# Second block: half the in-projection and all gate products dealt out by k steps between small products, the mask as contraction rows, the gate bias added by VectorE

## The chip, the cores and the metric

The kernel runs on one core of a Trainium2 chip, all in float32. Its time is the device time of the whole program in microseconds. Engines are TensorE (PE; PEld is its weight load), VectorE (DVE), ScalarE (ACT), GpSimd (POOL) and SyncE (SP).

## The reference

Two transformer blocks of depth 2 run one after the other on 256 tokens of width 1024. The first (adaptive norms, attention, a mixture of 32 experts) is untouched. Cut to what matters, a layer of the second is

```
h = rmsnorm(x, norm_g)
u_a, v_a, z_a, c_q, c_kv, k_r, z_b, q_c, k_c, v_c, g_c, z_c, gate_logits = split(h @ w_in)
y_a = gelu(u_a) * (mask(w_s) @ layernorm(gelu(v_a)) + b_s) * silu(z_a)
y_b = chunk_causal_attention(q(c_q), k(c_kv, k_r), v(c_kv)) * silu(z_b)      # 8 heads of 96
y_c = rmsnorm(gla(q_c, k_c, v_c, g_c)) * silu(z_c)                            # 4 heads, chunks of 64
gates = sigmoid(gate_logits + b_gate)                                         # 3 x 1024
x = x + (sum_n gates[n] * (y_n @ w_branch[n])) @ w_out
```

In y_b a query sees a key if the key's chunk of 64 is not later than its own.

## The kernel before

The 256 rows are two tiles of 128 (`LAT` = 2). A **unit** is one PSUM bank that TensorE fills and another engine takes: units A (`BANK_A`, three banks) are taken by ScalarE, units D (`BANK_D`, three) by VectorE, each ring in order. w_in and the other wide weights stream through a ring in SBUF: `stream` (L355 to L395) is the order, each item is 2 MB (a **chunk**: 1024 x 512, k-major in 8 slices), SyncE loads an item as soon as the last use of the item before it in its slot is done, and the second block uses `SLOTS2` = 4 of the six slots. The other two hold the opened gates `GS` and, on two partitions, the bias `BG`. Chunks 0, 1 and 2 of the eight in-projection chunks (`IN_CHUNKS`, the last 432 wide) give u_a, v_a and z_a, chunk 3 c_q, c_kv, k_r and the start of z_b.

TensorE's program of a layer (from L899) is written out by hand and sets the order of everything:

- in-projection (L906): 8 chunks x 2 tiles, a unit of 8 matmuls each (L912). A float32 matmul appears in the trace as two passes, so a unit is 16 rows of PE.
- rows: the spatial weight turned (L921), then gate units (L893, and L895 for the bias) and the spatial product (L928); for each tile the normalised latents are turned (L936, L937) and multiplied (L941, L942, L945), two gate units follow, and the heads' rows are turned (L951).
- heads: for each tile 8 heads in a pipeline of ten rounds: score (L961) with the chunk mask added by a product of the identity and a constant (L962), the probabilities' transposition (L969) one round later and the product with V (L979) two rounds later.
- GLA for each tile: L987 to L1036, with two of the gate units between.
- branches: one or two gate units, then for each branch the rows turned (L1048) and multiplied by w_branch (L1057); then the out-projection (L497, L1073).

In all 12 gate units of `gates` (L882):

```python
for k in range(KD):
    nc.tensor.matmul(u[:, :], HT2[:, k, tile * P:(tile + 1) * P], w[:, k, :], start=(k == 0), stop=False)
q, b0 = 32 * (c // BRANCHES), c % BRANCHES * 512
nc.tensor.matmul(u[:, :], C("ones")[q:q + 1, :].to_broadcast([1, P]), BG[q:q + 1, b0:b0 + 512], start=False,
                 stop=True).then_inc(s_unitA, 1)
```

ScalarE (from L1266) copies in-projection units, does Gelu, Silu, the square roots (L1109), the heads' exponentials (L1297) and opens each gate unit with a Sigmoid (L1264). VectorE (from L1935) normalises (L1956 to L2028), takes the maxima of the scores (L2041, L2043), copies what was turned (L2033, L2046) and adds up the branches (L2137 to L2142). POOL issues the layer's vector loads (L2300 to L2315).

## Time and profile before

| | |
|---|---|
| median of 3 runs | 2511.5 us (2511.03 to 2512.53) |
| profiled execution | 2511.9 us, span 2510.0 us |
| PE busy | 2068.1 us (82%) |
| DVE, ACT busy | 602.1 us (24%), 394.4 us (16%) |
| second block, layer 0 (first in-projection product to last branch product) | 1701.67 to 2065.42 |
| second block, layer 1 | 2107.48 to 2472.40 |

PE busy counts pipelined matmuls, with modelled ends: durations of neighbours overlap, so the pitch of a sequence is the difference of two starts. A bracket in a timeline row is the time in which the engine stood idle before that row, and who released it. PEclk is the TensorE clock that was granted, 1.00 for 2.4 GHz.

### The profile page before, as it was taken

The numbers are of one execution on the slowest core, as the hardware profiler recorded it, in microseconds if no ns is written. First come the engines' busy times: TensorE is split into PE (matmuls) and PEld (weight loads), VectorE is DVE, ScalarE is ACT, GpSimd is POOL, SyncE is SP. The second block draws the span as 40 slices with busy tenths as digits, with TensorE's granted clock in tenths as the row PEclk, the third lists the DMA queues.
The fourth block names the chain that finished last, engine by engine and source line by source line (L and its number), as shares of the span: only waits on it lengthen the run. The fifth ranks groups of instructions, "written<-read, shape, count | busy, mean of one in ns | idle before, by whom it ended". The sixth has DMA issues, their size and how long they took to land.

```text
span 2510.0 us, 20024 instructions
## 1 busy us (share of the span) xinstructions
PE 2068.1 (82%) x8105; PEld 958.4 (38%) x8105; DVE 602.1 (24%) x1340; ACT 394.4 (16%) x815; POOL 100.0 (4%) x148
## 2 busy tenths in 40 slices
PE   5999987778777776896877777759988899998898
PEld 1444434333332233553333333214435444444543
DVE  1234425200000004744000000020055231035322
ACT  1122410100000002331000000011222211031310
POOL 1001000100000001001000000001000001000000
PEclk8999998899999988997999998989988899998789
DMA  9257552799999997205999999966411134431020
GB/s 351 99 188 264 190 199 109 294 428 428 427 428 427 428 425 283 101 26 200 425 428 428 427 429 427 428 277 237 162 67 42 67 123 151 143 120 67 34 95 23
DMA packets 119727, 620.90 MB, mean 247 GB/s; under 512 B 8016, under 2 KB 10336, under 8 KB 95056
## 3 DMA queue, kind: packets, MB, share of 16 engines
q1 hardware_dynamic: 101664, 561.04, 55.6%
q0 software_dynamic: 12208, 37.54, 4.3%
q10 hardware_dynamic: 5760, 20.97, 2.2%
q8 instruction: 69, 1.13, 0.2%
q14 instruction: 26, 0.21, 0.0%
HBM read 594.30 MB, written 25.23 MB: 247 GB/s over the span
## 4 chain that ended last, share of the span: by engine, by line
PE 57%; DMA 31%; DVE 7%; ACT 2%; issue 2%; SPq 1%; ACTq 0%; POOL 0%; DVEq 0%; POOLq 0%
DMA ring<-in_w_up 28%; PE bank L680 11%; PE bank L912 9%; PE bank L893 7%; PE bank L760 5%; PE bank L1057 3%; PE bank L550 3%; PE bank L1073 2%; PE bank L814 2%; PE bank L634 2%; PE bank L610 1%; PE bank L497 1%; PE bank L895 1%; DMA ring<-in_w_ada 1%; DMA big<-mod_d 1%
## 5 line engine op out<-in xcount | busy, mean ns | idle before, releaser
L680 PE MATMUL bank<-ring,big 128*64 128x512 f32 x3072 | 743.8, 640 | 207.2 <-DMA ring<-in_w_gate 95.8
L680 PEld LDWEIGHTS bank<-ring,big 128*64 128x64 f32 x3072 | 261.0, 147 | 665.3 <-issue 630.0
L912 PE MATMUL bank<-ring,big 128*128 128x512 f32 (+1 forms) x512 | 220.1, 593 | 1.7 <-issue 1.7
L893 PE MATMUL bank<-ring,big 128*128 128x512 f32 x384 | 185.2, 639 | 0.0
L1885 DVE TENSOR_TENSOR big<-big,bank 128x512 f32<-128x512 f32 x32 | 22.0, 688 | 660.9 <-PE bank L680 660.9
L912 PEld LDWEIGHTS bank<-ring,big 128*128 128x128 f32 x512 | 98.7, 193 | 122.4 <-issue 122.4
L760 PE MATMUL bank<-ring,big 128*128 128x512 f32 x320 | 140.7, 599 | 0.0
L1091 ACT ACTIVATE big<-bank 128x512 f32<-128x512 f32 (+3 forms) x102 | 57.5, 576 | 461.1 <-PE bank L912 204.4
L893 PEld LDWEIGHTS bank<-ring,big 128*128 128x128 f32 x384 | 77.1, 206 | 99.7 <-issue 99.4
L497 PE MATMUL bank<-cst,big 128*128 128x128 f32 x176 | 31.5, 349 | 77.1 <-DVE big L1940 30.9
L1057 PE MATMUL bank<-ring,big 128*128 128x512 f32 x192 | 85.7, 605 | 4.4 <-ACT big L1091 4.4
L760 PEld LDWEIGHTS bank<-ring,big 128*128 128x128 f32 x320 | 61.0, 193 | 74.2 <-issue 74.2
L814 PE MATMUL bank<-ring,big 128*128 128x512 f32 x192 | 85.8, 602 | 0.0
L1890 DVE COPY big<-bank 128x512 f32<-128x512 f32 x32 | 22.1, 692 | 259.6 <-PE bank L680 259.6
L550 PE MATMUL bank<-ring,small 128*2 128x512 f32 x160 | 73.9, 593 | 8.1 <-DVE big L1392 7.8
L1213 ACT ACTIVATE big<-bank 128x512 f32<-128x512 f32 x32 | 19.1, 597 | 355.9 <-PE bank L672 355.9
L1218 ACT ACTIVATE big<-bank 128x512 f32<-128x512 f32 x32 | 19.1, 597 | 351.9 <-PE bank L680 351.9
L551 PE MATMUL bank<-ring,small 128*2 128x512 f32 x160 | 74.0, 593 | 0.0
L2243 POOL DMA_INDIRECT big<-h_d,slot_tok x32 | 30.8, 962 | 811.9 <-PE bank L672 772.0
L497 PEld LDWEIGHTS bank<-cst,big 128*128 128x128 f32 x176 | 27.5, 183 | 85.7 <-issue 51.9
L1177 ACT ACTIVATE big<-bank,small 128x512 f32<-128x512 f32 (+1 forms) x96 | 57.8, 612 | 6.2 <-DVE small L1538 6.2
L1226 ACT ACTIVATE big<-bank 128x512 f32<-128x512 f32 x32 | 19.1, 597 | 244.3 <-PE bank L680 244.3
(382 smaller groups left out, 1940.7 us busy)
## 6 DMA issues: line engine op xcount, KB each, us to landing
ring<-in_w_gate SPq DMA_DIRECT2D x64, 2048.0 KB, 18.4
ring<-in_w_up SPq DMA_DIRECT2D x64, 2048.0 KB, 19.9
ring<-in_w_down SPq DMA_DIRECT2D x64, 2048.0 KB, 19.6
ring<-in_w_in SPq DMA_DIRECT2D x26, 2048.0 KB, 7.8
ring<-in_w_ada SPq DMA_DIRECT2D x24, 2048.0 KB, 13.7
y_d<-big ACTq DMA_DIRECT2D x32, 512.0 KB, 10.3
ring<-in_w_qkv SPq DMA_DIRECT2D x6, 2048.0 KB, 19.9
ring<-in_w_branch SPq DMA_DIRECT2D x6, 2048.0 KB, 7.6
```

Source lines behind the costliest of these rows:

```text
L497: ins = nc.tensor.transpose(u[:, k * P:(k + 1) * P], rows[:, c:c + P], ident)
L550: nc.tensor.matmul(bank[0:2, :], cT[:, i, :], w0[:, i * 512:(i + 1) * 512], start=(i == 0), stop=(i == KD - 1))
L551: ins = nc.tensor.matmul(bank[64:66, :], cT[:, i, :], w1[:, i * 512:(i + 1) * 512], start=(i == 0), stop=(i == KD - 1))
L634: ins = nc.tensor.matmul(banks[6][64 * r:64 * r + 64, 0:256], ROWS[:, kt, v0:v0 + HD], PT(n)[:, i // 2, i % 2, 256 * r:256 * r + 256], sta ...
L680: ins = nc.tensor.matmul(bank[half * CAP:(half + 1) * CAP, :], lhs[:, k, half * CAP:(half + 1) * CAP], w[:, k * step + c0:k * step + c0 + ...
L760: ins = nc.tensor.matmul(u[:, :], hT(tile, k), w[:, k, :], start=(k == 0), stop=(k == KD - 1))
L814: ins = nc.tensor.matmul(u[:, :], hT(tile, k), wo[c][:, k, :], start=(k == 0), stop=(k == KD - 1))
L893: nc.tensor.matmul(u[:, :], HT2[:, k, tile * P:(tile + 1) * P], w[:, k, :], start=(k == 0), stop=False)
L912: ins = nc.tensor.matmul(u[:, 0:n], HT2[:, k, tile * P:(tile + 1) * P], w[:, k, :], start=(k == 0), stop=(k == KD - 1))
L1057: ins = nc.tensor.matmul(u[:, :], YT[:, k, tile * P:(tile + 1) * P], w[:, k, c * 512:(c + 1) * 512], start=(k == 0), stop=(k == 3))
L1091: nc.scalar.activation(dst, src, ACT.Copy, scale=scale).then_inc(s_outA, 1)
L1177: ins = nc.scalar.activation(pr[:, i * n:(i + 1) * n], sc[r][:, i * n:(i + 1) * n], ACT.Exp, bias=nm[:, h:h + 1], accum_out=rs[:, h:h + 1])
```

## The change

Of the in-projection, chunks 0, 1, 3 and 2 (in this order) stay whole units; the later four and all 12 gate units become **beside units**: a list `BESIDE` of 20 units, 160 steps of one k slice (one matmul, two passes). `beside(layer, n)` issues the next n steps wherever it is called, and the table `POINTS` says how many: 18 and 20 ahead of the turned heads, 4 (tile 0) or 3 (tile 1) a head, 4 to 10 at five places of GLA in either tile. Beside units have two banks of their own (`BANK_F`: the third of A, and one that only the first block used); units A of the second block go down to two banks. ScalarE copies the in-projection's beside units, VectorE adds the bias (now a broadcast of 128 x 3072 in SBUF) to the gates' ones, and ScalarE opens them later in place, 1024 wide. The bias products are gone.

The chunk mask becomes two more contraction rows of scores: `KMT` and `QMT` grow from 96 to 98 partitions, filled by three small DMAs on POOL's queue, and the mask product is gone. The latents of both tiles are normalised ahead of the spatial product, the gating of the spatial rows moves into tile 0's latents, Silu is done in three places, the branches' rows are turned earlier into two buffers, and the weight ring has three slots, since `BG` needs the room.

```diff
-SLOTS2 = 4
+SLOTS2 = 3
...
-        KMT = xc[0:MQK, :, :]...
+        MQX = MQK + LAT
+        KMT = xc[0:MQX, :, :]...
...
+        BG = spare[:, LAT * BRANCHES * D:(LAT + 1) * BRANCHES * D]
+        BANK_F = (banks[2], banks[7])
...
+        IN_ORDER = (0, 1, 3, 2, 4, 5, 6, 7)
+        BESIDE = [("in", *IN_CHUNKS[i], tile) for i in IN_ORDER[4:] for tile in range(LAT)]
+        BESIDE += [("gate", c, 512, tile) for c in range(2 * BRANCHES) for tile in range(LAT)]
...
+        POINTS = {"rows": (18, 20), "heads": (4, 3), "decay": (4, 6), "logs": (9, 10), "exps": (9, 9),
+                  "turned": (4, 4), "states": (6, 5)}
+        def bank_a(n):
+            return BANK_A[n % 3] if n < marks["second"] else BANK_A[(n - marks["second"]) % 2]
...
+            def beside(layer, steps):
+                for _ in range(steps):
+                    m, k = made[0] // KD % len(BESIDE), made[0] % KD
+                    n = made[0] // KD
+                    made[0] += 1
+                    kind, c, cols, tile = BESIDE[m]
+                    w, at_ = weights((kind, layer, c))
+                    u = BANK_F[n % 2]
+                    if k == 0 and n >= 2:
+                        pe.wait_ge(*beside_taken(n - 2))
+                    ins = nc.tensor.matmul(u[:, 0:cols], HT2[:, k, tile * P:(tile + 1) * P], ...
+                                           start=(k == 0), stop=(k == KD - 1))
...
-                    gates(layer, 2 - tile)
...
+                for i in (0, 1):
                     for tile in range(LAT):
+                        in_unit(layer, i, tile)
...
+                for tile in range(LAT):
+                    in_unit(layer, 3, tile)
+                spatial(0)
+                in_unit(layer, 2, 0)
+                spatial(1)
+                turned_at = latents_turn(0)
+                in_unit(layer, 2, 1)
+                pe.wait_ge(s_outA, turned_at)
+                latents_out()
+                turned_at = latents_turn(1)
+                beside(layer, POINTS["rows"][0])
+                heads_turn()
+                pe.wait_ge(s_outA, turned_at)
+                latents_out()
+                beside(layer, POINTS["rows"][1])
+                heads_turn()
                 taken("D")
+                pe.wait_ge(s_mask, 48 * (layer + 1))
...
-                            nc.tensor.matmul(u[:, n - P:n], ident, C("chunk"), start=False, stop=True,
-                                                  skip_group_check=True).then_inc(s_unitA, 1)
...
+                        if s < MH:
+                            beside(layer, POINTS["heads"][tile])
...
+                branches_at.append(branch_turn(1))
+                branch(layer, 0, branches_at[0])
+                branch(layer, 1, branches_at[1])
+                pe.wait_ge(s_dp, due(s_dp))
+                branches_at.append(branch_turn(2))
+                branch(layer, 2, branches_at[2])
...
+                    if kind == "in":
+                        act.wait_ge(s_fin, i + 1)
+                        nc.scalar.activation(PROJ[:, tile, c:c + cols], BANK_F[i % 2][:, 0:cols], ACT.Copy).then_inc(s_finA, 1)
...
+            def open_gates(layer, n):
+                act.wait_ge(s_finD, BESIDE_GATES * layer + 2 * LAT * (n + 1))
+                for tile in range(LAT):
+                    v = GS[tile][:, n * D:(n + 1) * D]
+                    nc.scalar.activation(v, v, ACT.Sigmoid).then_inc(s_sig, 1)
...
+                    if kind == "gate":
+                        dve.wait_ge(s_fin, i + 1)
+                        V.tensor_tensor(GS[tile][:, c * 512:(c + 1) * 512], BANK_F[i % 2], BG[:, c * 512:(c + 1) * 512],
+                                        ALU.add).then_inc(s_finD, 1)
...
-                dve.wait_ge(s_silus, due(s_silus, 3 * LAT))
...
+                    if tile == 0:
+                        dve.wait_ge(s_silus, due(s_silus, LAT))
+                        for i in range(LAT):
+                            uu = PROJ[:, i, C_U:C_U + BW]
+                            V.tensor_tensor(uu, uu, PROJ[:, i, C_ZA:C_ZA + BW], ALU.mult).then_inc(s_sgd, one(s_sgd))
...
+                load_vector(BG, t["b_gate_2"][layer], s_bg)
+                mask = t["consts"][:, CONST:CONST + MASK]
+                pool.wait_ge(s_h, marks["rows", layer])
+                pool.dma_start(KMT[MQK:MQX, :, :].rearrange("p h n -> p (h n)"), mask[0:LAT, :]).then_inc(s_mask, 16)
+                pool.wait_ge(s_sgd, LAT * (layer + 1))
+                for i in range(LAT):
+                    pool.dma_start(QMT[i][MQK:MQX, :, :].rearrange("p h n -> p (h n)"),
+                                   mask[LAT * (i + 1):LAT * (i + 2), 0:MH * P]).then_inc(s_mask, 16)
```

**TensorE, heads of tile 0.** L961 and L1044 are the scores, L962 the mask, L969 and L1050 the transposition, L979 and L1060 the product with V, L919 a beside step. Before:

```order
L961 MATMUL bank<-xc,big 128x128 [waits unit_taken_by_scalar]
L962 MATMUL bank<-cst 128x128
L969 MATMUL bank<-cst,big 128x128 [waits unit_taken_by_vector,unit_taken_by_scalar]
L979 MATMUL bank<-big 128x64 [waits o_unit_taken,unit_taken_by_vector]
L961 MATMUL bank<-xc,big 128x128 [waits unit_taken_by_scalar]
```

and now:

```order
L1044 MATMUL bank<-xc,big 128x128 [waits unit_taken_by_scalar]
L1050 MATMUL bank<-cst,big 128x128 [waits unit_taken_by_vector,unit_taken_by_scalar]
L1060 MATMUL bank<-big 128x64 [waits o_unit_taken,unit_taken_by_vector]
L919 MATMUL bank<-ring,big 128x512 [waits weights_slot0] x2
L919 MATMUL bank<-ring,big 128x432 [waits beside_unit_taken_by_scalar,weights_slot1]
L919 MATMUL bank<-ring,big 128x432 [waits weights_slot1]
L1044 MATMUL bank<-xc,big 128x128 [waits unit_taken_by_scalar]
```

A head is followed by four steps; the mask product is gone; a beside unit can begin in the middle of them, and there TensorE waits for ScalarE's copy of the unit two before.

**TensorE, tile 0 from the latents to the turned heads.** L936 to L945 and L953 to L965 are the latents, L893, L895 a gate unit, L951 and L973 the turned heads. Before, behind the latents' products:

```order
L893 MATMUL bank<-ring,big 128x512 [waits unit_taken_by_scalar,weights_slot1]
L893 MATMUL bank<-ring,big 128x512 x7
L895 MATMUL bank<-ring,cst 128x512
L893 MATMUL bank<-ring,big 128x512 [waits unit_taken_by_scalar,weights_slot2]
L893 MATMUL bank<-ring,big 128x512 x7
L895 MATMUL bank<-ring,cst 128x512
L951 MATMUL bank<-cst,big 96x128 [waits unit_taken_by_vector,vector_result_for_tensor]
L951 MATMUL bank<-cst,big 96x128 x3
L951 MATMUL bank<-cst,big 96x128 [waits unit_taken_by_vector]
```

and now, with the next tile's latents turned first:

```order
L953 MATMUL bank<-cst,big 128x128 [waits unit_taken_by_scalar,vector_result_for_tensor]
L953 MATMUL bank<-cst,big 128x128
L954 MATMUL bank<-cst,big 128x128
L919 MATMUL bank<-ring,big 128x512 [waits weights_slot1] x16
L919 MATMUL bank<-ring,big 128x512 [waits beside_unit_taken_by_scalar,weights_slot2]
L919 MATMUL bank<-ring,big 128x512 [waits weights_slot2]
L973 MATMUL bank<-cst,big 96x128 [waits unit_taken_by_vector,vector_result_for_tensor]
L973 MATMUL bank<-cst,big 96x128 x3
```

Two whole gate units with bias became 18 steps, and the next tile's turning of latents moved ahead of them.

**VectorE, heads of tile 1.** L2169 and L2171 are maximum and negation, L2174 the copy of the turned probabilities, L2052 the bias's add, all in VectorE's order. Before (L2041, L2043, L2046 there):

```order
L2041 TENSOR_REDUCE small<-bank 128x1 [waits unit_for_scalar]
L2043 TENSOR_SCALAR small<-small 128x1 [waits vector_chain]
L2046 COPY big<-bank 128x256 [waits unit_for_vector]
L2041 TENSOR_REDUCE small<-bank 128x1 [waits unit_for_scalar]
L2043 TENSOR_SCALAR small<-small 128x1 [waits vector_chain]
```

and now:

```order
L2169 TENSOR_REDUCE small<-bank 128x1 [waits unit_for_scalar]
L2171 TENSOR_SCALAR small<-small 128x1 [waits vector_chain]
L2174 COPY big<-bank 128x256 [waits unit_for_vector]
L2052 TENSOR_TENSOR ring<-bank,ring 128x512 [waits beside_unit_ready]
L2169 TENSOR_REDUCE small<-bank 128x1 [waits unit_for_scalar]
```

The add stands behind a head's copy and ahead of the next head's maximum; it waits for the beside unit that ends in the steps between them.

## Rows read from the trace of the kernel before

**Rows 1.** The page: TensorE's granted clock in 40 slices of 62.75 us.
```profile
PEclk8999998899999988997999998989988899998789
```

**Rows 2.** Windows by stage: length, busy us and instructions per engine, PEclk, DMA.
```profile
1811.44:1900.10 88.66, 77.91 (x209) 35.55 (x207) 48.56 (x93) 25.00 (x34) 0.00 (x0) 0.92 0.28 95
1900.10:1932.90 32.80, 26.39 (x137) 23.96 (x137) 15.54 (x54) 9.32 (x33) 0.00 (x0) 0.74 0.00 1
1932.90:2010.25 77.35, 67.08 (x220) 36.51 (x219) 22.00 (x54) 22.23 (x32) 0.54 (x1) 0.80 0.17 61
2010.25:2065.42 55.17, 52.96 (x139) 23.97 (x138) 17.12 (x29) 5.33 (x9) 0.00 (x0) 1.00 0.33 114
...
sum 363.75, PE 334.10 PEld 169.46 DVE 103.29 ACT 70.77 POOL 0.54; mean PE 66.82 PEld 33.89 DVE 20.66 ACT 14.15 POOL 0.11
...
sum 364.92, PE 335.28 PEld 168.48 DVE 103.30 ACT 70.78 POOL 0.00; mean PE 67.06 PEld 33.70 DVE 20.66 ACT 14.16 POOL 0.00
...
1932.90:2010.25 77.35, 35.35 (x64) 14.60 (x64) 0.80 0.17 61
```

**Rows 3.** Timeline, PE, first gate units: start, us, instructions [idle before <- releaser].
```profile
1811.88 7.03 PE L893 MATMUL bank<-ring,big 128*128 128x512 f32 x16
1818.84 1.12 PE L895 MATMUL bank<-ring,cst 1*128 1x512 f32 x2
1819.89 0.70 PE L893 MATMUL bank<-ring,big 128*128 128x512 f32 x1
```

**Rows 4.** Timeline, PE, latents of tile 0; then DVE's last write of that chain.
```profile
1843.46 0.69 PE L936 MATMUL bank<-cst,big 128*128 128x128 f32 x2 [5.29 <-DVE big L1991]
1844.94 2.07 PE L941 MATMUL bank<-big 128*128 128x512 f32 x2 [0.58 <-ACT big L1091]
...
1849.62 1.88 PE L945 MATMUL bank<-big 128*128 128x512 f32 x4
1851.34 1.88 PE L893 MATMUL bank<-ring,big 128*128 128x512 f32 x4
...
1862.85 0.42 DVE L2028 TENSOR_TENSOR big<-big 128x256 f32<-128x256 f32 x1
```

**Rows 5.** Timeline, PE, heads of layer 0.
```profile
1901.33 0.49 PE L961 MATMUL bank<-xc,big 96*128 96x128 f32 x2 [1.15 <-DVE xc L2033]
...
1904.44 0.47 PE L969 MATMUL bank<-cst,big 128*128 128x128 f32 x1 [1.96 <-ACT big L1297]
...
1910.52 0.44 PE L961 MATMUL bank<-xc,big 96*128 96x128 f32 x2
1910.79 0.39 PE L962 MATMUL bank<-cst 128*128 128x128 f32 x2
1911.38 0.33 PE L969 MATMUL bank<-cst,big 128*128 128x128 f32 x1 [0.20 <-ACT big L1297]
...
1911.72 0.44 PE L961 MATMUL bank<-xc,big 96*128 96x128 f32 x2
```

**Rows 6.** Timeline, PE, GLA of layer 0, and a full-speed product of the rows stage.
```profile
1951.34 1.05 PE L1008 MATMUL bank<-cst,big 128*64 128x128 f32 x4 [2.74 <-DVE big L2084]
...
1953.95 2.05 PE L1018 MATMUL bank<-big 64*128 64x128 f32 x8 [0.70 <-ACT big L1091]
...
1828.01 1.16 PE L928 MATMUL bank<-big 128*128 128x128 f32 x8
```

**Rows 7.** First block, dealt filling: timeline, PE, and the window around it.
```profile
153.34 0.59 PE L550 MATMUL bank<-ring,small 128*2 128x512 f32 x1
...
153.87 0.70 PE L587 MATMUL bank<-big 64*128 64x256 f32 x4
...
150.00:165.00 15.00, 13.52 (x74) 5.13 (x76) 6.67 (x13) 5.76 (x17) 0.00 (x0) 1.00 0.13 34
```

**Rows 8.** The page: a group of VectorE (busy us, mean ns), and a DMA group.
```profile
L1885 DVE TENSOR_TENSOR big<-big,bank 128x512 f32<-128x512 f32 x32 | 22.0, 688 | 660.9 <-PE bank L680 660.9
...
ring<-in_w_in SPq DMA_DIRECT2D x26, 2048.0 KB, 7.8
```

More of the change, by code:

```diff
@@ new lines, in in_unit @@
+            def in_unit(layer, i, tile):
+                c0, n = IN_CHUNKS[i]
+                w, at_ = weights(("in", layer, c0))
+                w = w[:, 0:KD * n].rearrange("p (k n) -> p k n", k=KD)
+                u = unit("A")
+                for k in range(KD):
+                    ins = nc.tensor.matmul(u[:, 0:n], HT2[:, k, tile * P:(tile + 1) * P], w[:, k, :],
+                                           start=(k == 0), stop=(k == KD - 1))
+                ins.then_inc(s_unitA, 1)
+                release(at_, "A")
+                marks["in", layer, i, tile] = count["A"]
@@ new lines, in spatial, with latents_turn @@
+            def spatial(tile):
+                pe.wait_ge(s_dp, due(s_dp))
+                u = unit("D")
+                for g in range(SG_GROUPS):
+                    ins = nc.tensor.matmul(u[:, g * P:(g + 1) * P], SGT[:, g, :], row(tile, C_V + g * P, P),
+                                           start=True, stop=True)
+                ins.then_inc(s_unitD, 1)
+            def latents_turn(tile):
+                pe.wait_ge(s_dp, due(s_dp))
+                u = unit("A")
+                for k in range(2):
+                    nc.tensor.transpose(u[:, k * P:(k + 1) * P], row(tile, C_CQ + k * P, P), ident)
+                nc.tensor.transpose(u[:, 2 * P:3 * P], row(tile, C_CKV, P), ident).then_inc(s_unitA, 1)
+                return count["A"]
@@ new lines, in branch @@
+            def branch(layer, n, turned_at):
+                pe.wait_ge(s_outA, turned_at)
+                w, at_ = weights(("branch", layer, n))
+                w = w.rearrange("p (k n) -> p k n", k=4)
+                for tile in range(LAT):
+                    for c in range(2):
+                        u = unit("D")
+                        for k in range(4):
+                            ins = nc.tensor.matmul(u[:, :], YT[n % 2][:, k, tile * P:(tile + 1) * P], w[:, k, c * 512:(c + 1) * 512],
+                                                   start=(k == 0), stop=(k == 3))
+                        ins.then_inc(s_unitD, 1)
+                release(at_, "D")
@@ L987, in _ @@
                     nc.tensor.transpose(u[0:GR, 0:P], row(tile, C_G, GR), ident).then_inc(s_unitA, 1)
+                    beside(layer, POINTS["decay"][tile])
                     taken("A")
@@ L1004, in _ @@
                     ins.then_inc(s_unitD, 1)
+                    beside(layer, POINTS["exps"][tile])
                     pe.wait_ge(s_dp, due(s_dp))
@@ L1013, in _ @@
                     ins.then_inc(s_unitA, 1)
+                    beside(layer, POINTS["turned"][tile])
                     taken("A")
@@ L1298, in _ @@
                                              accum_out=rs[:, h:h + 1]).then_inc(s_outA, 1)
+                        beside(layer, POINTS["heads"][tile])
+                act.wait_ge(s_finA, BESIDE_IN * (layer + 1))
+                silu_rows(C_ZC)
                 for tile in range(LAT):
@@ L1992, in _ @@
                     dve.wait_ge(s_dp, so_far(s_dp))
+                for tile in range(LAT):
+                    u = take()
+                    for g in range(SG_GROUPS):
+                        uu = PROJ[:, tile, C_U + g * P:C_U + (g + 1) * P]
+                        ins = V.scalar_tensor_tensor(uu, u[:, g * P:(g + 1) * P], SGB[:, g:g + 1], uu, ALU.add, ALU.mult)
+                    ins.then_inc(s_outD, one(s_outD))
+                    dve.wait_ge(s_outD, so_far(s_outD))
+                for tile in range(LAT):
                     u = take()
@@ L2070, in _ @@
                     dve.wait_ge(s_dp, so_far(s_dp))
+                    beside(layer, POINTS["logs"][tile])
                     u = take()
@@ L2085, in _ @@
                     dve.wait_ge(s_dp, so_far(s_dp))
+                    beside(layer, POINTS["exps"][tile])
                     u = take()
@@ L2090, in _ @@
                     V.tensor_copy(QZ[:, 1, :, 64:P], qg[:, :, 64:P]).then_inc(s_outD, one(s_outD))
+                    beside(layer, POINTS["turned"][tile])
                     u = take()
@@ L2107, in _ @@
                     V.memset(mark(), 0.0).then_inc(s_dp, one(s_dp))
+                    beside(layer, POINTS["states"][tile])
                     u = take()
```

280 lines of the change are left out of this document (139 added, 141 removed).

## The prediction

> **What bounds the kernel now.** I read these views in this order. The page shows the TensorE clock in 40 slices: 9 tenths and more (2.4 GHz) in most slices, with dips in the second block's thirteen that only a half-speed level (1.2 GHz) in part of a slice can make [rows 1]. So there are two things to look for, waits of TensorE and half-speed stretches. The windows by stage then give both at once for layer 0: a stage's length minus its PE busy time is TensorE's waiting, and the clock column says how fast it ran. After the in-projection come four stages: "rows" (88.66 us, 77.91 busy, clock 0.92), "heads" (32.80, 26.39 busy, 0.74), "GLA" (77.35, 67.08 busy, 0.80) and "branches" (55.17, 52.96 busy, 1.00) [rows 2]. TensorE therefore waits 10.75 + 6.41 + 10.27 + 2.21 = 29.6 us in a layer, and it works at half speed in much of the two middle stages. No weight load ends a wait: w_in lands in 7.8 us [rows 8], while a chunk of two units keeps TensorE 14 us. The bound is TensorE in program order, and what can be won is waiting, half-speed time and superfluous products. Layer 1 repeats it: 364.92 against 363.75 us from the first in-projection product to the last branch product [rows 2].
>
> **The parts of the change, per layer.**
>
> *Gate bias products, removed.* Each of 12 gate units ended with a one-row bias product. It starts at 1818.84 and the next unit at 1819.89, 1.05 us [rows 3]: 12 x 1.05 = 12.6 us off the path. The add goes to VectorE, 12 of 128x512 from PSUM, about 0.69 us each by the same shape in the first block [rows 8]. VectorE has that time: eight steps of filling take 6.9 us, and the beside units use banks of their own, so an add may be a whole unit late before TensorE notices. If that cover is gone, an add costs its 0.69.
>
> *Waits in the rows stage.* The waits are for VectorE's normalisations (5.29 us is the first [rows 4]) and sum to 10.75 us [rows 2]. Four in-projection units now stand between the chains, and 18 and 20 steps (0.43 us a pass at L945's full-speed pitch, two passes a step, so 0.86 us: 15.5 and 17.2 us) stand ahead of the two turnings of heads. What must be covered there is VectorE's chain from the latents' last product (1849.62 + 1.88 = 1851.50) to its last write (1863.27): 11.8 us [rows 4], plus 1.4 us for two gating products that now lie inside the first one: 13.2 against 15.5. I take the 10.75 as gone. The latents' own products run at half speed after that wait: 6.40 us from 1844.94 to 1851.34, where at the speed of L945 (four passes of 512 in 1.72) eight such passes and four half passes are 4.3 [rows 4]. Twice 2.1 is 4.2 us.
>
> *Heads.* Of 32.80 us little is work. A full-speed head of tile 0 has score 0.27 (1910.52 to 1910.79), transposition 0.17 and value product 0.17 (0.34 for the two from 1911.38 to 1911.72): 0.61 [rows 5]. A head of tile 1 has twice of each, at most 1.22. Eight of each are 14.6 us. The wait for the last copied rows (1.15 [rows 5]) stays, since nothing is dealt behind it, and so does some 0.5 us at each tile's last two rounds, which have no steps: 16.8 us in all, so 16.0 saved, mask products included. The mask rides in two more contraction rows, which cost no column. Four or three steps (3.4 or 2.6 us) lie between score and use; before, TensorE stood 1.96 us at the first head for an exponential with its table load [rows 5], and that is the longest.
>
> *GLA.* The waits, 10.27 us, have 4 to 10 steps (3.4 to 8.6 us) in front of each, against 2.74 us for the longest shown [rows 6]: gone. The four gate units here take 35.35 us where 4 x 7.03 = 28.1 is full speed [rows 2, 3]: 7.2 saved. The small products gain too, if the clock holds. L1018's 8 passes took 2.05 us, where L928's 8, of twice the depth, take 1.16 [rows 6]. Nothing is the least; the most is the stage's clock loss, 0.20 x 77.35 = 15.5, less the 7.2: 8.3. I take 5.0, between them, since the small stretches already at full speed there gain nothing.
>
> *Branches.* Two of the three waits for turned rows go (2.2 us of idle for three): 1.5 us [rows 2].
>
> *What is added.* Small products now stand behind wide ones 28 times a layer. The first block is already dealt out so: its last filling product starts at 153.34, the next score product at 153.87, 0.53 after a product whose pitch is 0.43 [rows 7]. That is 0.1 each, 2.8 us; bounds 0 and twice that. The mask rows' DMAs (three of 8 or 16 KB) and the bias of 1.5 MB are issued on POOL's queue behind the layer's vectors, ahead of the next layer's norm gain; the mask rows go when the spatial rows are gated, some 40 us ahead of the heads, and the others have more. The ring loses its fourth slot; each load then still has two chunks, 27 us, in front of its use, against 7.8 us. The six sigmoids of 128x1024 go beside the last GLA steps. All at nothing.
>
> Sum: 12.6 + 10.8 + 4.2 + 16.0 + 10.3 + 7.2 + 5.0 + 1.5 - 2.8 = 64.8 us a layer, 129.6 in two. The profiled execution took 2511.9 us (span 2510.0), the median is 2511.5; 2511.9 - 129.6 = 2382.3, so **2382 us**.
>
> **Will the clock hold?** The row that speaks for it is from the first block, where two-column products of 512 rows fill the gaps between heads: its window 150 to 165 us has clock 1.00 with 13.52 of 15 us busy [rows 7]. Against it, the Trainium skill, "TensorE: Matmul & The Clock Gate", Part 4, says that a transposition does not count as busy for the clock gate in the way a matmul does; the heads and GLA stages hold many. By the rule they would stay at half speed in part; the trace agrees only in that the stretch of heads without wide products ran at 0.74, and the first block's window, where the heads' transpositions stand between the fills too, speaks against it for dealt-out work.
>
> **Rivals.**
> *The clock stays as low as it is (5%).* The mechanism is the one just told. Heads become 56 steps x 0.86 + 16.8 = 65 us, GLA 66 steps x 0.86 + about 23 = 80 us. At mean clocks of 0.74 to 0.80, 145 us lose some 23%, 33 us a layer; the time would be 2382 + 66 = 2448. For it: the row of heads. Against: wide products are now four fifths of either stage.
> *The steps do not cover the chains (12%).* VectorE's and ScalarE's queues are in order, and each got new work ahead of what TensorE waits for: an add or copy waits for its beside unit, with reduces and copies of the next head queued behind it, and table loads for Silu between heads. If half of the 29.6 us returns, the time is 2382 + 30 = 2412. For it: the margin of 13.2 against 15.5. Against: the banks give each unit a slack of eight steps.
> *Slower, by the weight ring (1%).* With three slots a load begins only when the chunk three back is done. If loads took longer than two chunks (27 us), each of the 19 of a layer would expose the rest; all 65 us are lost at 27 + 65/19 = 30.5 us a load, four times the 7.8 seen, and past it the kernel is slower (at 35 us: 2382 + 2 x 19 x 8 = 2686). The bias's broadcast shares the engines, but once a layer and 1.5 MB only.
> *The change does nothing (1%).* The order might leave the waits where they are because the small products are dependent in other ways. Even then 24 bias products go: 2487.
>
> **How the numbers follow.** The forecast case has 80%, the rivals 19%, and 1% is left for what I don't see. Inside the forecast case the unknown costs reach from 5.0 to 8.3 in GLA's small products and 2.8 to 0 for the changes of width (6 us a layer less: 2370) to nothing gained in the small products and twice the switching (7.8 us more: 2398). Stretched over most of the second rival, the range is 2370 to 2410. A measurement of this kernel tells 0.2%, 5 us, from no change. Faster by more than that 0.97, within it 0.01, slower 0.02.
>
> **What would show it.** Right: heads about 65 us a layer with 56 wide steps in them at clock 1.00, GLA about 80 with gate units of 6.9 us, idle of TensorE under 6 us a layer after the in-projection, first in-projection product to last branch product near 299 us instead of 364. Wrong: a clock under 0.95 in heads or GLA; waits over 1 us ending in VectorE at L1044, L1050 or L1096; a beside step that waits for a weight slot; or a layer's length over 312 us.

## The result, and the profile after

The changed kernel takes 2361.5 us in the median of 4 runs (2359.73 to 2363.17), the kernel before 2512.0 (2511.03 to 2512.85): a ratio of 0.9401 (95% interval 0.9385 to 0.9417), 150.5 us less. The forecast was 2382 with a range of 2370 to 2410. The direction and the mechanism were right, the size was not: the time lies 8.5 us below the range. The profiled execution took 2359.7 us with a span of 2357.9, against 2511.9 before, so the two traces differ by 152.2 us.

The page of the kernel after; the PEclk line answers to [rows 1]:

```profile
PE 1977.6 (84%) x7993; PEld 910.3 (39%) x7993; DVE 618.1 (26%) x1364; ACT 376.4 (16%) x791; POOL 102.5 (4%) x152
...
PEclk9999999699899998799698989899799999999999
```

The last eleven slices of PEclk, which are the second block's, have no dip left. PE's busy time fell by 90 us, which is less than the 152 us won: the rest was waiting.

Windows by stage of the kernel after, with the columns of [rows 2]: rows (from the first in-projection product, since half the in-projection is now dealt out), heads, GLA and branches of layer 0, and then layer 1 up to the out-projection:

```profile
1701.11:1804.52 103.41, 103.36 (x286) 49.39 (x286) 48.72 (x94) 19.89 (x31) 1.13 (x3) 1.00 0.48 171
1804.52:1865.71 61.19, 59.70 (x216) 33.90 (x217) 17.30 (x57) 14.05 (x40) 0.00 (x0) 1.00 0.30 104
1865.71:1944.34 78.63, 78.63 (x289) 41.63 (x288) 28.19 (x63) 22.26 (x32) 0.56 (x1) 1.00 0.37 129
1944.34:1990.21 45.87, 43.43 (x113) 19.83 (x112) 18.57 (x32) 5.55 (x8) 0.00 (x0) 1.00 0.32 113
2030.57:2322.03 291.46, 287.48 (x901) 145.69 (x901) 112.76 (x245) 61.76 (x111) 1.16 (x3) 0.99 0.36 126
```

Every stage of layer 0 runs at clock 1.00 (2.4 GHz), layer 1 at 0.99 since its in-projection begins at half speed, and in the GLA stage TensorE is busy for all of its 78.63 us. From the first in-projection product to the end of the last branch product, layer 0 takes 287.4 us (1701.11 to 1988.5) instead of 363.8: 76.4 less. Layer 1, taken to the transposition that opens the out-projection, takes 291.5 instead of 366.6 (2107.48 to 2474.11): 75.2 less. 0.6 us lie outside.

Timeline of PE, rows stage (start, us, instructions; a bracket is the idle time before a row). These answer to [rows 3, 4]:

```profile
1743.72 7.03 PE L933 MATMUL bank<-ring,big 128*128 128x512 f32 x16
1750.59 1.05 PE L944 MATMUL bank<-big 128*128 128x128 f32 x8
...
1758.68 1.02 PE L961 MATMUL bank<-big 128*128 128x512 f32 x2
...
1761.26 1.88 PE L965 MATMUL bank<-big 128*128 128x512 f32 x4
...
1763.30 15.62 PE L919 MATMUL bank<-ring,big 128*128 128x512 f32 x36
1778.75 2.09 PE L973 MATMUL bank<-cst,big 128*96 128x128 f32 x16
```

A unit's pitch without a bias product is 6.87 us (1743.72 to 1750.59). The latents of tile 0 take 4.29 us from their first product to the next work (1758.68 to 1762.97) where they took 6.40. Behind them, 18 steps keep TensorE 15.45 us, and the turning of heads at L973 doesn't wait. VectorE's chain in that cover, first and last row on DVE:

```profile
1763.90 1.29 DVE L2125 TENSOR_TENSOR big<-big 128x512 f32<-128x512 f32 x2
...
1775.81 0.42 DVE L2154 TENSOR_TENSOR big<-big 128x256 f32<-128x256 f32 x1
```

It ends at 1776.23, 13.1 us after the latents' last product (1761.26 + 1.88). The forecast had 13.2 against 15.5.

Heads, PE, answering to [rows 5]: the start of tile 0, one head in full, the one other wait (between the tiles), and a head of tile 1:

```profile
1805.67 0.49 PE L1044 MATMUL bank<-xc,big 98*128 98x128 f32 x2 [1.15 <-DVE xc L2159]
1805.99 3.60 PE L919 MATMUL bank<-ring,big 128*128 128x512 f32 x8
...
1813.20 0.39 PE L1044 MATMUL bank<-xc,big 98*128 98x128 f32 x2
1813.42 0.27 PE L1050 MATMUL bank<-cst,big 128*128 128x128 f32 x1
1813.53 0.33 PE L1060 MATMUL bank<-big 128*128 128x64 f32 x2
1813.70 3.39 PE L919 MATMUL bank<-ring,big 128*128 128x512 f32 x8
...
1835.68 0.43 PE L1060 MATMUL bank<-big 128*128 128x64 f32 x2 [0.21 <-DVE big L2174]
...
1839.67 2.74 PE L919 MATMUL bank<-ring,big 128*128 128x512 f32 x6
1842.24 0.60 PE L1044 MATMUL bank<-xc,big 98*128 98x256 f32 x2
...
1843.29 2.79 PE L919 MATMUL bank<-ring,big 128*128 128x512 f32 x6
1845.92 0.60 PE L1044 MATMUL bank<-xc,big 98*128 98x256 f32 x2
```

A head of tile 0 costs 0.50 us of its own between steps (1813.20 to 1813.70), a head of tile 1 1.05. The transposition (L1050) has a pitch of 0.11, where 0.17 was read before. A score of two passes has 0.22 (1813.20 to 1813.42), where 0.27 was read; but that 0.05 is only borne by another now. Six wide passes take 2.63 behind a value product (1843.29 to 1845.92) and 2.57 behind a transposition (1839.67 to 1842.24), so what stands first behind a value product is some 0.05 longer, be it a score or a step. No step waits anywhere.

GLA, PE, answering to [rows 6]; and branches with the out-projection:

```profile
1888.05 0.60 PE L1096 MATMUL bank<-cst,big 128*64 128x128 f32 x4
...
1892.45 1.16 PE L1107 MATMUL bank<-big 64*128 64x128 f32 x8
...
1974.51 14.00 PE L997 MATMUL bank<-ring,big 128*128 128x512 f32 x32 [0.74 <-ACT big L1167]
1990.21 1.97 PE L523 MATMUL bank<-cst,big 128*128 128x128 f32 x16 [1.71 <-DVE small L2282]
```

L1096 took 1.05 and waited 2.74 us before, L1107 took 2.05 as L1018. Inside a layer three waits are left: 1.15, 0.21 and 0.74 (the 1.71 in the last row stands ahead of the out-projection, as before).

The bias went to VectorE as the group `L2052`, 24 adds of 692 ns; TensorE waits for none of them:

```profile
L2052 DVE TENSOR_TENSOR ring<-bank,ring 128x512 f32<-128x512 f32 x24 | 16.6, 692 | 24.2 <-PE bank L919 23.6 <-DVE big L2204 0.2
```

### The profile page after: what moved, and what is told of

The parts are those of the page before. It is cut to its first block, busy times and chain, and to the rows that moved or that the text cites. A ratio compares the mean times of both kernels' runs of the same rounds, so it can differ in the third digit from the quotient of the medians.

```text
span 2357.9 us, 19834 instructions
## 1 busy us (share of the span) xinstructions
PE 1977.6 (84%) x7993; PEld 910.3 (39%) x7993; DVE 618.1 (26%) x1364; ACT 376.4 (16%) x791; POOL 102.5 (4%) x152
## 4 chain that ended last, share of the span: by engine, by line
PE 59%; DMA 31%; DVE 6%; issue 1%; ACT 1%; SPq 1%; ACTq 0%; POOL 0%; DVEq 0%; POOLq 0%
DMA ring<-in_w_up 29%; PE bank L706 13%; PE bank L919 12%; PE bank L786 6%; PE bank L933 5%; PE bank L997 4%; PE bank L576 3%; PE bank L1149 2%; PE bank L840 2%; PE bank L660 2%; PE bank L636 1%; PE bank L523 1%; DMA ring<-in_w_ada 1%; PE bank L613 1%; DMA big<-mod_d 1%
## 5 line engine op out<-in xcount | busy, mean ns | idle before, releaser
L706 PE MATMUL bank<-ring,big 128*64 128x512 f32 x3072 | 753.2, 647 | 198.5 <-DMA ring<-in_w_gate 87.1
L919 PE MATMUL bank<-ring,big 128*128 128x512 f32 (+1 forms) x640 | 282.2, 590 | 0.0
L919 PEld LDWEIGHTS bank<-ring,big 128*128 128x128 f32 x640 | 117.5, 190 | 126.2 <-issue 126.1
L786 PE MATMUL bank<-ring,big 128*128 128x512 f32 x320 | 140.1, 597 | 0.0
L933 PE MATMUL bank<-ring,big 128*128 128x512 f32 x256 | 113.7, 603 | 1.7 <-issue 1.7
L1167 ACT ACTIVATE big<-bank 128x512 f32<-128x512 f32 (+1 forms) x86 | 48.2, 575 | 350.8 <-PE bank L786 103.4
L786 PEld LDWEIGHTS bank<-ring,big 128*128 128x128 f32 x320 | 60.8, 192 | 73.9 <-issue 73.9
L840 PE MATMUL bank<-ring,big 128*128 128x512 f32 x192 | 86.0, 603 | 0.0
L997 PE MATMUL bank<-ring,big 128*128 128x512 f32 x192 | 83.3, 593 | 1.5 <-ACT big L1167 1.5
L933 PEld LDWEIGHTS bank<-ring,big 128*128 128x128 f32 x256 | 48.9, 194 | 61.2 <-issue 61.2
## 6 DMA issues: line engine op xcount, KB each, us to landing
y_d<-big ACTq DMA_DIRECT2D x32, 512.0 KB, 10.3
```

Source lines behind the costliest of these rows:

```text
L706: ins = nc.tensor.matmul(bank[half * CAP:(half + 1) * CAP, :], lhs[:, k, half * CAP:(half + 1) * CAP], w[:, k * step + c0:k * step + c0 + ...
L786: ins = nc.tensor.matmul(u[:, :], hT(tile, k), w[:, k, :], start=(k == 0), stop=(k == KD - 1))
L840: ins = nc.tensor.matmul(u[:, :], hT(tile, k), wo[c][:, k, :], start=(k == 0), stop=(k == KD - 1))
L919: ins = nc.tensor.matmul(u[:, 0:cols], HT2[:, k, tile * P:(tile + 1) * P], w[:, 0:KD * cols].rearrange("p (k n) -> p k n", k=KD)[:, k, :], ...
L933: ins = nc.tensor.matmul(u[:, 0:n], HT2[:, k, tile * P:(tile + 1) * P], w[:, k, :], start=(k == 0), stop=(k == KD - 1))
L997: ins = nc.tensor.matmul(u[:, :], YT[n % 2][:, k, tile * P:(tile + 1) * P], w[:, k, c * 512:(c + 1) * 512], start=(k == 0), stop=(k == 3))
```

## The experiments

All but the last start from the changed kernel. Each ratio is to the kernel before, timed on the same chip.

**The changed kernel again.**

> The changed kernel once more, as the base of the runs beside it. Every theory: 2361 us within 2 us.

Measured: 2360.2 us, ratio 0.9398 (0.9382 to 0.9414). It serves as the base, and it showed something unexpected: its layer 0 is 291.2 us to the out-projection, not 289.1 as in the first trace, since it began at half speed. Windows of the first 8 us of the in-projection of layer 0, by kernel (columns as above, clock third from the end). First the kernel after in its first trace, then the same kernel again:

```profile
1701.00:1705.00 4.00, 3.89 (x9) 1.82 (x10) 0.01 (x1) 0.00 (x0) 0.13 (x1) 1.00 0.94 274
1705.00:1709.00 4.00, 4.00 (x11) 1.79 (x10) 0.00 (x0) 0.60 (x1) 0.00 (x0) 1.00 1.03 376
```

```profile
1701.00:1705.00 4.00, 4.00 (x5) 1.53 (x5) 0.00 (x0) 0.00 (x0) 0.00 (x0) 0.51 0.95 321
1705.00:1709.00 4.00, 4.00 (x11) 1.82 (x10) 0.00 (x0) 0.00 (x0) 0.00 (x0) 1.00 1.02 386
```

The same code, after a pause of 25 to 26 us both times, starts once at 2.4 and once at 1.2 GHz. 1.9 of the 76.4 us of layer 0 are this, and not the change.

**The bias as a product again.**

```diff
+                    if kind == "gate" and k == KD - 1:
+                        ...
+                        ins = nc.tensor.matmul(u[:, :], C("ones")[0:1, :].to_broadcast([1, P]), BG[0:1, c * 512:(c + 1) * 512],
+                                               start=False, stop=True)
...
-                        V.tensor_tensor(GS[tile][:, c * 512:(c + 1) * 512], BANK_F[i % 2], BG[:, c * 512:(c + 1) * 512],
-                                        ALU.add).then_inc(s_finD, 1)
+                        V.tensor_copy(GS[tile][:, c * 512:(c + 1) * 512], BANK_F[i % 2]).then_inc(s_finD, 1)
```

> Changed kernel, but each gate unit ends with the one-row bias product again and VectorE only copies. My sum: 12 x 1.05 = 12.6 us a layer, 25 us in all, so 2386 to 2388. Rival (a one-row product behind a wide one hides part of itself, as the small products now seem to): clearly less, 2375 to 2380. Rival (VectorE's add was on the path): less than 25 too, with waits of TensorE for the beside units gone.

Measured: 2389.9 us, ratio 0.9517 (0.9501 to 0.9533), 29.7 more than the base: 24 products of 1.24 us. They are paid in full, and nothing hides them. Timeline of PE, one of them among steps:

```profile
1873.14 1.88 PE L919 MATMUL bank<-ring,big 128*128 128x512 f32 x4
1874.96 1.12 PE L925 MATMUL bank<-ring,cst 1*128 1x512 f32 x2
1876.01 1.98 PE L919 MATMUL bank<-ring,big 128*128 128x512 f32 x4
```

From its start to the next step are 1.05 us, as I had read it before the change; but the step ahead of it has become longer too, 1.82 us for four passes where 1.72 is the pitch of wide work. The passes behind it are longer as well: in the kernel before, a unit between two bias products takes 8.12 us with its own (1819.89 to 1828.01, [rows 3, 6]), where 6.87 is the unit alone, 1.25 more. A cost read from start to start misses what the instruction does to its neighbours. VectorE's copy in place of the add takes 691 ns, the add 692, so the add itself is free.

**The mask as a product again.** The identity and the mask constant make a second product behind each score.

```diff
-                            nc.tensor.matmul(u[:, 0:n], QMT[tile][:, s, :], KMT[:, s, 0:n], start=True, stop=True).then_inc(s_unitA, 1)
+                            nc.tensor.matmul(u[:, 0:n], QMT[tile][0:MQK, s, :], KMT[0:MQK, s, 0:n], start=True, stop=True)
+                            nc.tensor.matmul(u[:, n - P:n], ident, C("chunk"), start=False, stop=True,
+                                                  skip_group_check=True).then_inc(s_unitA, 1)
```

> Changed kernel, but the mask is a product of identity and constant again and the two mask rows are left out of the scores. If a small product costs here what it cost in the heads of the kernel before at full speed (0.22 us for two passes): 32 x 0.22 = 7.0, 2368. If a pass in the wake of a wide product costs only its columns (128 in 0.05 us): 32 x 0.11 = 3.5, 2365. If the product was hidden anyway: 2361.

Measured: 2368.3 us, ratio 0.943 (0.9414 to 0.9446), 8.1 more than the base: 32 products of 0.25. Timeline of PE, a head of tile 0:

```profile
1815.74 0.39 PE L1044 MATMUL bank<-xc,big 96*128 96x128 f32 x2
1815.96 0.39 PE L1045 MATMUL bank<-cst 128*128 128x128 f32 x2
1816.18 0.27 PE L1052 MATMUL bank<-cst,big 128*128 128x128 f32 x1
1816.29 0.33 PE L1062 MATMUL bank<-big 128*128 128x64 f32 x2
```

The score alone has the same 0.22 at 96 and at 98 rows, so the two mask rows are free. The product is paid in full: the cheap passes in the wake of wide work, for which 2365 was expected, are not seen. And the transposition behind the small mask product has a pitch of 0.11 (1816.18 to 1816.29), as it has in the changed kernel behind a score. So what made it 0.17 in the rows read before was not that its neighbours were small; it had a wait of 0.20 right ahead of it [rows 5].

**A ring of two slots.** `SLOTS2 = 3` becomes `SLOTS2 = 2`.

> Changed kernel with a ring of two slots in place of three in the second block: a load starts one chunk (14 us) ahead of its use. If a load of 2 MB takes 8 us as the page says, nothing changes: 2361 to 2364, with at most a wait where a chunk of branches or the first chunk of layer 1 comes close. If the ring is near its limit (the rival on which a slower kernel rested), 28 loads are exposed by some us each: over 2400.

Measured: 2362.2 us, ratio 0.9409 (0.9394 to 0.9425), and no wait of TensorE in the layers ends in a weight load. With even one slot fewer than the change left, the time is 2.0 us above the base and 0.7 above the changed kernel's first median, which may be nothing. The slower rival is excluded with its mechanism.

**Heads without steps.** The 56 steps of the heads' stage go elsewhere, and the total stays 160.

```diff
-POINTS = {"rows": (18, 20), "heads": (4, 3), "decay": (4, 6), "logs": (9, 10), "exps": (9, 9),
-          "turned": (4, 4), "states": (6, 5)}
+POINTS = {"rows": (30, 34), "heads": (0, 0), "decay": (14, 16), "logs": (9, 10), "exps": (9, 9),
+          "turned": (4, 4), "states": (11, 10)}
```

> Changed kernel with no beside steps between the heads; the 56 steps lie at other places (rows 30 and 34, first and last place of GLA 14, 16 and 11, 10), so that the work is the same. Heads took 32.8 us before and take 15.3 us of their own now. If dealing is what pays (waits of the exponentials covered, clock kept): 32.8 less the mask products (16 at 0.25, 4.0) is 28.8, 13.5 us a layer more, 27 us, 2388, with a granted clock near 0.75 in the heads. If the clock and the short heads come from elsewhere (banks, mask rows, Silu moved): under 2370.

Measured: 2393.3 us, ratio 0.9521 (0.9506 to 0.9536), 32 to 33 more than the base. Windows of the heads' stage of both layers, and the timeline of PE in layer 0: the first wait of either tile for an exponential, and one late head:

```profile
1825.91:1855.21 29.30, 23.69 (x105) 18.75 (x106) 15.41 (x54) 11.88 (x37) 0.00 (x0) 0.65 0.18 69
2171.55:2203.70 32.15, 26.76 (x104) 22.46 (x105) 15.43 (x54) 12.53 (x38) 0.00 (x0) 0.58 0.16 62
```

```profile
1830.02 0.47 PE L1050 MATMUL bank<-cst,big 128*128 128x128 f32 x1 [2.25 <-ACT big L1402]
...
1842.57 0.69 PE L1050 MATMUL bank<-cst,big 128*128 128x128 f32 x2 [1.07 <-ACT big L1402]
...
1850.41 0.65 PE L1044 MATMUL bank<-xc,big 98*128 98x256 f32 x2
...
1851.74 0.65 PE L1044 MATMUL bank<-xc,big 98*128 98x256 f32 x2
```

A stage that costs 15.3 us of its own (with its first wait, steps taken off at their full-speed pitch) when steps lie in it costs 29.3 and 32.2 when bare. Of the 14.0 more in layer 0, 4.0 are waits for exponentials (2.25, 0.38, 1.07 and 0.51, where 0.21 is left otherwise). The other 10.0 go with a clock of 0.65, but are not all of its making: at full speed, too, a bare head of tile 1 takes 1.33 us (1850.41 to 1851.74) against 1.05 beside steps, and one of tile 0 0.61 [rows 5] against 0.50. For eight heads of each that is 3.1 us, my estimate of what short waits without a bracket and first products behind a wait cost; some 7 are left for the clock. The mask is in the contraction rows here too. So of the 17.5 us that heads gained in layer 0, 3.5 are the mask products (32.8 before against 29.3 bare, though at clocks of 0.74 and 0.65), 4.0 the waits shown, some 3 the hidden ones and some 7 the clock.

**The same steps in one block.** All of a tile's steps behind head 3.

```diff
-                        if s < MH:
-                            beside(layer, POINTS["heads"][tile])
+                        if s == 3:
+                            beside(layer, MH * POINTS["heads"][tile])
```

> Changed kernel, the same number of steps in the heads of a tile, but all 32 (24) behind round 3 in one block. Covered waits only: every round but one has its wait again, as with no steps, so nearly the 27 us of the bare heads come back (2383 to 2388). Clock only: the block of 27 us keeps the clock up for the rounds behind it, the three rounds ahead of it are few, so under half of it (2366 to 2374). This tells what part of the dealing's gain is wait and what part clock.

Measured: 2387.4 us, ratio 0.9505 (0.949 to 0.9519), 27 more than the base. Timeline of PE: the wait for the first exponential, the block, and a wait long behind it.

```profile
1809.84 0.48 PE L1050 MATMUL bank<-cst,big 128*128 128x128 f32 x1 [2.25 <-ACT big L1402]
...
1812.51 27.63 PE L919 MATMUL bank<-ring,big 128*128 128x512 f32 x64
...
1841.49 0.33 PE L1050 MATMUL bank<-cst,big 128*128 128x128 f32 x1 [0.57 <-ACT big L1402]
1841.66 0.33 PE L1060 MATMUL bank<-big 128*128 128x64 f32 x2
...
1844.04 0.48 PE L1050 MATMUL bank<-cst,big 128*128 128x128 f32 x1 [0.15 <-ACT big L1402]
```

Shortly behind the block a transposition has its full-speed pitch of 0.17 (1841.49 to 1841.66); at 1844, after four heads and three waits, a transposition takes 0.48 again. Nearly as much is lost as with no steps at all, and the block itself begins at half speed (clock 0.79 from 1812.5 to 1822.5). So it isn't the quantity of wide work in the stage but its place between the small products that takes away the waits and holds the clock. How the 27 us divide between the two this run doesn't tell.

**Twice as many groups of steps in the heads.** Half of a head's steps behind its score, half behind its value product: 16 more places a layer where small products stand behind wide ones, 32 in all.

```diff
+                            beside(layer, POINTS["heads"][tile] // 2)
...
-                            beside(layer, POINTS["heads"][tile])
+                            beside(layer, POINTS["heads"][tile] - POINTS["heads"][tile] // 2)
```

> Changed kernel, a head's steps split in two (2 + 2, 1 + 2): half behind the score, half behind the V product, so twice as many changes between wide and small products, same work. My forecast's price of 0.1 us a change: 32 more changes, 3.2 us, 2364.7. If a small product in the wake of a wide one is cheaper, since its weight load is hidden: a head gets 0.05 to 0.1 us shorter, 1.5 to 3 us less, 2359. If neither, no change.

Measured: 2360.8 us, ratio 0.9399 (0.9385 to 0.9414), that is 0.7 less than the changed kernel's first median and 0.6 more than its second. Timeline of PE:

```profile
1811.31 1.88 PE L919 MATMUL bank<-ring,big 128*128 128x512 f32 x4
1813.03 0.27 PE L1051 MATMUL bank<-cst,big 128*128 128x128 f32 x1
1813.14 1.88 PE L919 MATMUL bank<-ring,big 128*128 128x512 f32 x4
```

Four wide passes keep their 1.72, and the transposition between two wide groups takes 0.11. A change of width costs nothing that can be told: 32 more places are worth -0.7 to +0.6 us, where the forecast's 0.1 each gives 3.2, and that price is refuted.

**The last two waits.** Three of the steps ahead of the second turning of heads go behind it, and the third branch's rows are turned ahead of the second branch's products.

```diff
-                beside(layer, POINTS["rows"][1])
+                beside(layer, POINTS["rows"][1] - 3)
                 heads_turn()
+                beside(layer, 3)
...
-                branch(layer, 1, branches_at[1])
                 pe.wait_ge(s_dp, due(s_dp))
                 branches_at.append(branch_turn(2))
+                branch(layer, 1, branches_at[1])
```

> Attempt at a better one: three of the 20 steps moved behind the second turning of heads (ahead of the wait for its copies, 1.15 us), and the third branch's rows turned ahead of the second branch's products (0.74 us). If both waits go: 1.9 us a layer, 3.8 us, 2357.7. If the wait for the copies only moves to the first head's exponential: 1.5 us in all, 2360.

Measured: 2353.8 us (2353.38 to 2354.7), ratio 0.9371 (0.9359 to 0.9384). It beats both kernels, the changed one by 6.4 to 7.7 us. Timeline of PE, layer 0's end and layer 1's start:

```profile
1960.28 27.63 PE L997 MATMUL bank<-ring,big 128*128 128x512 f32 x64
...
2029.98 10.54 PE L933 MATMUL bank<-ring,big 128*128 128x512 f32 x24 [0.83 <-issue]
```

The last 64 passes of branch products run through. Its layer 1, to the out-projection, takes 286.7 us, begun at full speed, against 289.1 for a layer of the changed kernel begun so: 2.4 less for waits of 1.15 + 0.74 = 1.9 in brackets. From the layer's start to its first branch product 1.4 are won (244.15 to 242.73), from there to the out-projection 1.0 (44.95 to 43.95), so each wait had some 0.25 us more on it than its bracket says. Part of that is how a bracket is counted, from the modelled end of the row before: the turning of heads lasts 2.09 us in its row, but here the next step starts 1.93 behind its start (1801.67 to 1803.60). Another part is the first product behind a wait: the first score takes 0.32 (1805.67 to 1805.99) in the changed kernel and 0.23 here. That is 4.8 us in two layers; what lies beyond it is within what the start of a layer varies by, and this trace's layer 1 did begin at full speed.

**The kernel before without its bias products.** Only this run edits the kernel before; the gates' bias is then missing from the computation.

```diff
-                        nc.tensor.matmul(u[:, :], HT2[:, k, tile * P:(tile + 1) * P], w[:, k, :], start=(k == 0), stop=False)
-                    q, b0 = 32 * (c // BRANCHES), c % BRANCHES * 512
-                    nc.tensor.matmul(u[:, :], C("ones")[q:q + 1, :].to_broadcast([1, P]), BG[q:q + 1, b0:b0 + 512], start=False,
-                                     stop=True).then_inc(s_unitA, 1)
+                        ins = nc.tensor.matmul(u[:, :], HT2[:, k, tile * P:(tile + 1) * P], w[:, k, :], start=(k == 0), stop=(k == KD - 1))
+                    ins.then_inc(s_unitA, 1)
```

> The kernel before with the twelve one-row bias products of the second block's gate units left out in each layer (the gates' bias is left out of the computation); nothing else is changed. Theory that such a product is paid in full wherever it stands, since each is a wide pass pair of its own: two layers x 12 x 1.14 us = 27.4 us less, about 2484 us, the same that the change gains by it and that its return to the changed kernel cost (29.7). Rival, that the gate units in the GLA stage are paced by what follows them in the order (the small products' waits), so that 8 of the 12 are partly hidden there: 10 to 18 us less, 2494 to 2502 us. The clock's two levels stay where they were in the heads and in GLA.

Measured: 2477.1 us, ratio 0.986 (0.9844 to 0.9877), 33.9 less than before. Neither expectation holds: more is won than was read as the products' cost. The windows say where the rest is. The last third of layer 0's heads, in the kernel before and in this one:

```profile
1920.00:1932.90 12.90, 12.23 (x64) 11.12 (x64) 5.57 (x19) 3.39 (x12) 0.00 (x0) 0.71 0.00 1
```

```profile
1911.00:1920.04 9.04, 8.31 (x60) 7.23 (x59) 5.16 (x18) 3.23 (x12) 0.00 (x0) 1.00 0.01 2
```

The heads of the kernel without bias products come back to full speed and stay there, and take 27.4 us instead of 31.6 (27.5 instead of 30.2 in layer 1): 6.8 us in all. Nothing in the heads' code was edited, only what stands ahead of them. It isn't the same everywhere. The rows stage, with 7 of a layer's 12 products, is 9.0 and 8.8 us shorter: two units fall from 16.1 to 13.7, that is 1.2 a product, and some of the latents run faster. GLA, with 4, is only 3.1 and 3.6 shorter, less than the products' 4.8, for its clock fell from 0.80 to 0.77 in both layers. Branches, with 1, are 1.2 and 2.8 shorter, the second by its clock as well. These add up, within 0.3, to the 35.0 us between the two traces. So taking the products out moved the clock up in one stage and down in the next; why, isn't settled by this run. It does show that the heads' waits and small products alone do not fix the clock: the last third has nearly the same of both (0.54 and 0.50 us of waiting), no wide product at all, and runs once at 0.71 and once at 1.00.

## Why the prediction was right and wrong

The mechanism held at each of its points. The idle time inside a layer is 2.1 us where under 6 was forecast; heads take 61.2 us (about 65; 16 of their 56 steps are 432 wide, 2.1 us less, which the forecast of the stage left out), GLA 78.6 (about 80), both at clock 1.00; gate units have 6.87 us (6.9); no step waits for a slot or a bank. What failed is the sum. By terms, in us for layer 0, with what the traces show:

| term | forecast | measured | from |
|---|---|---|---|
| bias products | 12.6 | 13.7 | unit period 8.01 before, 6.87 after |
| waits in rows | 10.8 | 10.8 | none left |
| latents and turnings | 4.2 | 6.1 | 6.40 to 4.29 and 6.53 to 4.37, the rest mostly in their turnings, which no longer run slow behind a wait |
| heads | 16.0 | 17.5 | 32.8 before, 15.3 beside the steps now |
| waits in GLA | 10.3 | 10.3 | none left |
| gate units in GLA | 7.2 | 7.9 | 35.35 against 4 x 6.87 |
| small products in GLA | 5.0 | 6.1 | 27.2 before, 21.1 now, without the branches' turning that moved in here |
| branches | 1.5 | 2.1 | one wait of 0.74 left |
| changes between wide and small | -2.8 | 0 | the split run |
| start of the in-projection | 0 | 1.9 | a start at full speed, by chance |
| sum | 64.8 | 76.4 | |

**The step that failed is the term of what is added, "That is 0.1 each, 2.8 us".** I read it from one start in the first block, whose steps are of another form. The split run puts 32 more such places in and the time stays, so the term measures 0 where 2.8 us a layer were taken off. It is the largest single miss, but only a quarter of the 11.6 us by which the sum is short. The rest is the second fault and, with 1.9, a start at full speed by chance.

**The second fault was that every small term was priced at its least.** The heads' own 16.8 us measure 15.3: the transposition was read as 0.17 right behind a wait of 0.20 [rows 5], where without one it takes 0.11, and two of them in a head of tile 1 were put at twice that. The bias product was read as 1.05 us from start to start. The period of a unit, 8.01 with and 6.87 without, gives 1.14 (1.25 where another bias product stands ahead), and its return to the changed kernel cost 1.24. Gate units were put at 7.03, which is a row's duration with its modelled end; the pitch is 6.87. The waits were taken at their brackets, and the run without the last two shows 0.25 more on each. None of it is over 2 us a layer, but all of it has one sign, and there are two layers: 64.8 against 76.4 is 23 us in both. The low end of the range took in only two of the terms, GLA's small products and the changes of width, as if all others were exact. That is why the range missed. The lucky start isn't what carried the time out of it: the changed kernel's second trace began both layers at half speed and took 2360.9.

**The bias term and the clock are not separate.** The run of the kernel before without bias products won 33.9 us, 6.8 of them in heads that were not edited, while GLA won less than its products cost. So a part of the heads' 17.5 would have come with the bias products' removal alone; the sum holds for the change as a whole, and not for each part done alone.

**The rivals.** That the clock stays low is excluded by the windows after, and the bare heads show that it would have been dear: 0.65 and 0.58 there. Here the Trainium skill, "TensorE: Matmul & The Clock Gate", Part 4, on transpositions that don't count as busy, had spoken against the change. The traces fit it no further than the bare stage: with the same transpositions and wide steps between them the clock is 1.00 in both layers. And in the kernel before without bias products the last third of the heads, with as many transpositions and no wide product, is at 1.00 too. That the steps don't cover the chains is excluded by the brackets, with 13.1 us of chain under 15.45 of cover; the block shows that this hangs on the place of the steps. The ring is excluded down to two slots. The 5, 12 and 1 in 100 for these were not too low, and my 0.97 for faster was right; only the range around the likeliest case was too narrow downwards.

**What stays open.** Why the clock fell in the heads of the kernel before: no run has the waits without the small products, and the run without bias products has both, in part at full speed. And what sets the clock at the start of a layer.

## What to carry to other kernels

Where small dependent products leave TensorE waiting and at half speed, deal independent wide work out between them, a few steps at each place; the same amount in one block gave back nearly all of it (27 of 33 us) in the heads here. A one-row product for a bias costs more than a full one of its columns (1.14 to 1.25 us against 0.86); VectorE adds the bias at no cost where it copies the bank anyway (692 against 691 ns). When forecasting, price an instruction by the period of a pattern with and without it, and let the range take in the error of all terms at once if they all round the same way.

## What the runs showed that I had not expected

- The clock at the start of the in-projection is not fixed by the kernel. After a pause of 25 to 26 us the first 4 us ran at 1.00 in one trace of the changed kernel and at 0.51 in the next. Of the nine others, the kernel before and the experiments, only the bare heads' layer 0 began at full speed too. The first two chunks (64 passes) take 27.7 to 30.1 us by it, so a layer varies by up to 2.4 us with the same code. The Trainium skill, "TensorE: Matmul & The Clock Gate", Part 1, says that how many matmuls run cold at a kernel's start differs from run to run; these traces show the same at a layer's start.
- As far as these rows show, a small product costs the same behind a score, behind a small mask product or between wide steps (a one-pass transposition 0.11 us), and more only right behind a wait (0.17) or, by 0.05, behind a value product. What looked like a gain from wide neighbours is the waits gone, the short ones without a bracket too.
- Taking 24 one-row products out of the kernel before made the heads, which were not edited, 4.1 and 2.7 us shorter by their clock, while GLA's clock fell from 0.80 to 0.77.
- A wait costs some 0.25 us more than its bracket: the bracket is counted from a modelled end (0.16 us late at the turning of heads), and the first product behind a wait is longer (0.32 against 0.23).
